# The norm that closes a wide feed-forward block, turned token tile by token tile, and the mixer's first projections taken slice by slice

## What is computed

```python
def _rms(x, g):
    xf = x.astype(jnp.float32)
    y = xf * lax.rsqrt(jnp.mean(xf * xf, axis=-1, keepdims=True) + EPS)
    return y.astype(x.dtype) * g

def _modulate(xn, shift, scale):
    return xn * (1.0 + scale) + shift
...
x = x + 0.5 * ml[:, 2] * _swiglu(_modulate(_rms(x, ffn1_norm[l]), ml[:, 0], ml[:, 1]), ffn1_w_in[l], ffn1_w_out[l])
h = h + 0.5 * mc[2] * _swiglu(_modulate(_rms(h, ffn1_norm[l]), mc[0], mc[1]), ffn1_w_in[l], ffn1_w_out[l])
y_c, y_l = _token_mix(_modulate(_rms(h, mix_norm[l]), mc[3], mc[4]),
                      _modulate(_rms(x, mix_norm[l]), ml[:, 3], ml[:, 4]),
                      mix_w_in[l], mix_b_in[l], ...)
```

## Time and profile before

| | |
|---|---|
| median of three timed runs | 2366.07 us (2363.42 to 2366.50) |
| span of the profiled execution | 2361.7 us |
| TensorE busy | 98% of the span |
| VectorE, ScalarE, GpSimd busy | 67%, 48%, 1% |
| DMA | 403.75 MB, 171 GB/s over the span |

### The profile page before, as it was taken

How to read it: one execution, slowest core, us unless ns; L and a number is a source line. 1 busy time by engine, 2 the same in 40 slices (tenths; PEclk the granted TensorE clock), 3 DMA queues, 4 the chain that set the end, 5 groups by cost and what they waited for, 6 DMA issues and landing times.

```text
span 2361.7 us, 32897 instructions
## 1 busy us (share of the span) xinstructions
PE 2319.4 (98%) x13270; PEld 1954.3 (83%) x13270; DVE 1584.7 (67%) x2393; ACT 1137.5 (48%) x1666; POOL 24.9 (1%) x65
## 2 busy tenths in 40 slices
PE   7999999999999999999999999999999999999998
PEld 4887887888888887888888888888888888888887
DVE  4677434657575777667776678676676676776766
ACT  4222223436434255445545468654464446875444
POOL 0001000010000000000000000000000000000000
PEclk9999999999999999999999999999999999999999
DMA  7468322434522234654555644455555555444553
GB/s 306 179 233 323 139 89 95 150 113 143 195 90 72 73 111 166 241 183 174 194 183 193 236 154 144 157 178 195 183 180 192 196 195 209 149 145 172 188 195 125
DMA packets 59311, 403.75 MB, mean 171 GB/s; under 512 B 8269, under 2 KB 8677, under 8 KB 11672
## 3 DMA queue, kind: packets, MB, share of 16 engines
q1 hardware_dynamic: 52704, 383.80, 45.3%
q10 hardware_dynamic: 4128, 9.95, 1.2%
q0 software_dynamic: 2336, 7.96, 1.1%
HBM read 400.60 MB, written 2.67 MB: 171 GB/s over the span
## 4 chain that ended last, share of the span: by engine, by line
PE 93%; DVE 3%; DMA 2%; ACT 1%; issue 1%; SPq 0%; DVEq 0%; ACTq 0%
PE pair L522 88%; DMA ring<-in_stream 2%; PE pair L904 1%; PE pair L620 1%; PE pair L1050 1%; DVE ring_parts L2346 1%; PE pair L853 0%; ACT xT L1533 0%; PE pair L1319 0%; PE pair L1334 0%; PE pair L892 0%; DVE rows L2463 0%; PE pair L1304 0%; DVE ring_parts L2336 0%; DVE X L2469 0%
## 5 line engine op out<-in xcount | busy, mean ns | idle before, releaser
L522 PE MATMUL pair<-xT_parts,ring_high 128*128 128x512 f32 x2112 | 747.6, 395 | 3.8 <-DVE xT_parts L2251 1.2
L522 PE MATMUL pair<-xT_parts,ring_parts 128*128 128x256 f32 (+2 forms) x2448 | 693.1, 298 | 4.7 <-DVE ring_parts L2346 3.1
L2336 DVE TENSOR_TENSOR ring_parts<-ring,ring_high 128x2048 fp32r<-128x2048 f32 x194 | 444.1, 2292 | 136.4 <-ACT ring_high L1590 136.3
L522 PEld LDWEIGHTS pair<-xT_parts,ring_parts 128*128 128x128 f32 (+1 forms) x2448 | 460.4, 188 | 45.8 <-issue 9.2
L522 PEld LDWEIGHTS pair<-xT_parts,ring_high 128*128 128x128 f32 x2112 | 384.5, 188 | 81.3 <-issue 2.0
L1590 ACT ACTIVATE ring_high<-ring 128x2048 fp32r<-128x2048 f32 x197 | 375.6, 1910 | 67.4 <-DMA ring<-in_stream 67.3
L2346 DVE TENSOR_TENSOR ring_parts<-ring,mix_high 128x1024 fp32r<-128x1024 f32 x144 | 169.2, 1218 | 37.5 <-ACT mix_high L1603 37.5
L1641 ACT ACTIVATE arena<-pair 128x512 f32<-128x512 f32 x110 | 65.6, 596 | 261.9 <-PE pair L522 261.9
L1603 ACT ACTIVATE mix_high<-ring 128x1024 fp32r<-128x1024 f32 x144 | 143.3, 1048 | 93.0 <-DMA ring<-in_stream 89.6
L522 PE MATMUL pair<-ring_parts,xT_parts 128*128 128x512 f32 (+1 forms) x448 | 173.9, 388 | 0.6 <-DVE ring_parts L2346 0.6
L522 PE MATMUL pair<-ring_parts,g_high 128*128 128x512 f32 x440 | 172.2, 391 | 0.2 <-issue 0.2
(11 more groups left out here) (432 smaller groups left out, 3863.6 us busy)
## 6 DMA issues: line engine op xcount, KB each, us to landing
ring<-in_stream SPq DMA_DIRECT2D x338, 1024.0 KB, 4.8
xn<-in_mods SPq DMA_DIRECT2D x14, 1024.0 KB, 4.8
arena<-in_mods SPq DMA_DIRECT2D x14, 1024.0 KB, 4.8
gateB<-gate_rows POOLq DMA_DIRECT2D x4, 512.0 KB, 7.6
xn<-maximum_rows POOLq DMA_DIRECT2D x8, 256.0 KB, 3.6
arena<-in_bT ACTq DMA_DIRECT2D x1, 1536.0 KB, 9.7
bias_scratch<-bias_row POOLq DMA_DIRECT2D x1, 1536.0 KB, 9.1
X<-in_x ACTq DMA_DIRECT2D x1, 1024.0 KB, 11.9
```

The source lines that it names most:

```text
L522: m = pe.matmul(o, l, r, start=start, stop=stop)
L2336: dve.tensor_tensor(out=ring_r[:, slot].rearrange("p a b -> p (a b)"), in0=w, in1=high[:, slot, :], op=ALU.subtract).then_inc(low_ready, 1)
```

## The change

What it does:

- TensorE turns the closing norm by token tile (`norm_wide_by_tile`). Tile 0's slices that land in free banks go first, as soon as tile 0's diagonal is there; those whose bank still held a down product follow with the next tiles. Tile 3 comes last, slice 0 to 7, and its matmuls raise `x_turned`.
- VectorE interleaves reciprocals and diagonals with the last updates: tile 0's behind update (1, 1) (second half row, tile 1), tile 1's behind (1, 2), tile 2's and tile 3's behind (1, 3).
- The high and low part of the mixer's first weight chunk are made before the updates, in the last step of the feed-forward part.
- Part 0 of the first projection group runs slice by slice, all four feature tiles for each slice, and waits for one more slice each time; for slice 0 it waits before each bank until ScalarE has read that bank.

```diff
+            def norm_wide_by_tile():
+
+                first = c.resid - 3
+                for t_, slices in enumerate((((0, 4), (0, 5), (0, 6), (0, 7), (0, 0), (0, 1)),
+                                             ((0, 2),) + tuple((1, k) for k in (4, 5, 6, 7, 0, 1, 2)),
+                                             ((0, 3), (1, 3)) + tuple((2, k) for k in range(KD)),
+                                             tuple((3, k) for k in range(KD)))):
+                    pe.wait_ge(rstd_done, c.rstd + t_ + 1)
+                    pe.wait_ge(resid, first + min(t_ + 1, 3))
+                    for u, k in slices:
+                        m = pe.matmul(bank[k][:, u * P:(u + 1) * P], X[:, u, k * P:(k + 1) * P], diag[:, u, :],
+                                      start=True, stop=True)
+                        if t_ == 3:
+                            m.then_inc(x_turned, 1)
+                        elif owed:
+                            m.then_inc(owed.pop(), 1)
+                c.rstd += 4
+                c.split += KD
...
-                pre_group(range(4), x=both, span=2 * S, turned=c.split, between=gates)
+                pre_group(range(4), x=both, span=2 * S, turned=c.split, between=gates, by_slice=True)
...
-                    if turned is not None:
+                    if turned is not None and (part or not by_slice):
                         pe.wait_ge(x_split, turned - (0 if part else 2 if span == S else CW))
-                    for b, at in fs:
+                    for k in range(CW if by_slice and part == 0 else 0):
+                        pe.wait_ge(x_split, turned - KD + k + 1)
+                        for n, (b, at) in enumerate(fs):
+                            if k == 0:
+                                pe.wait_ge(x_whole, turned - KD + n + 1)
+                            wl, wh = mix_weights(k, slice(at, at + rows), True)
+                            mm(b[0:rows, 0:span], wl, whole[:, k, 0:span], k == 0, False)
+                            mm(b[0:rows, 0:span], wh, rest[:, k, 0:span], False, False)
+                            mm(b[0:rows, 0:span], wh, whole[:, k, 0:span], False, False)
+                    for b, at in fs if part or not by_slice else ():
...
             ffn(4)
-            norm_wide()
+            norm_wide_by_tile()
...
+                        if i == FT // 2 - 1:
+                            mix_split(-1, 0)
...
-                 first_ahead, lambda: mix_split(-1, 0))
+                 first_ahead)
...
+            def diagonals(nt):
 
                 for t_ in rstds(nt):
                     dve.tensor_scalar(diag[:, t_, :], ident[:, :], rstd[:, t_:t_ + 1], None,
                                       ALU.mult).then_inc(rstd_done, 1)
+                    yield t_
...
+                        if i == FT // 2 - 1:
+                            mix_low(-1, 0)
...
+                rooted_tile = diagonals(nt)
                 for n in range(2):
                     for t_ in range(nt):
                         if (n, t_) == (1, 1):
...
                         update(t_, n, down_bank(nt, t_, n), None)
+                        if nt == 4 and n and t_:
+                            next(rooted_tile)
+                if nt == 4:
+                    next(rooted_tile)
...
-            norm(4, lambda: mix_low(-1, 0))
+            norm(4, rooted_before=True)
```

More of the change, by code:

```diff
@@ L1147, in pre_group @@
             def pre_group(features, tokens=(), rows=P, cols=None, width=N, x=None, span=S, turned=None, between=None,
-                          first=None, beside=None):
+                          first=None, beside=None, by_slice=False):
                 whole, rest = x or x_parts
@@ L2233, in rstds @@
                     yield t_
-            def norm(nt, ahead=None):
+            def diagonals(nt):
                 for t_ in rstds(nt):
@@ L2239, in norm @@
                                       ALU.mult).then_inc(rstd_done, 1)
+                    yield t_
+            def norm(nt, ahead=None, rooted_before=False):
+                for t_ in () if rooted_before else diagonals(nt):
+                    pass
                 if ahead:
```

## The result

| | before | after |
|---|---|---|
| median of 21 runs each, in turn on one chip | 2364.47 us | 2367.55 us |
| ratio (95% interval) | | 1.0016 (1.001 to 1.0022) |
| span of the profiled execution, its own time | 2361.7 | 2364.9, 2366.61 |

The change makes the kernel about 3 us slower. The forecast was 1.70 us faster; its range ended at 2367.4, and it gave "same" 0.88. The median lies just outside that range. The ratio's interval lies almost wholly within the 0.2% that the forecast called the limit of measurement, but with 21 runs on each side it excludes 1.

What follows compares the result with a forecast made beforehand. TensorE, 93% of the chain, bounds the kernel; only its 2.73 us idle at this boundary could be won. Projections starting at 416.47 instead of 418.17 save 1.70 us, taking 2366.07 to 2364.4 us; range 2361.2 to 2367.4.

Steps and rivals of the forecast that it cites:

- the gain is carried to the end: Once VectorE waits for TensorE again, by 433.1, all engines keep their distances and the 1.70 us won stays.
- Waiting for each slice costs nothing visible: Part 0 of the projections: slices follow every 1.06 us, TensorE uses 2.75 us for each, so it never waits again.
- The purse and the new order: Between last down products and projections TensorE idles 2.73 us; the new order starts projections at 416.47, not 418.17.
- Slice 0 was the limit: The norm ends at 415.45, but slice 0's low part holds the projections until 416.47.
- Either part alone: Norm by tile without slices one by one starts projections 1.4 us later than before; slice by slice alone wins nothing.
- `gates()` and the backlog: VectorE finishes the gate weights' low part by 425.95; TensorE wants it after part 0, at 427.47: margin 1.5 us.
- Rival 1: Later slices push VectorE's backlog into TensorE and the gain is swallowed: 2366.1 us, chance 0.12.
- Rival 2: Steps between VectorE and ScalarE run 0.3 to 0.5 us longer, so tiles 1 to 3 wait: 2365.4 us, chance 0.10.
- Rival 3: Slice 0 is there when the norm ends, winning the 2.73 us idle: 2363.3 us; chance 0.11 for more than 2.4.
- Rival 4: TensorE's clock falls to its lower level, part 0's 48 matmuls take 11.0 us more: 2375.4 us, chance 0.05.
- the 4.4 us "around" the span: Time outside the profiled span of 2361.7 us, taken as untouched, leading to the median of 2366.07 us.
- later waits for weights that grow by what was won: Sign of a wrong forecast: later in the program, TensorE's waits for weights grow by the 1.70 us gained.

Runs made afterwards that it cites:

- before_8w: Kernel before plus 16 TensorE waits on a value long reached (8 instructions) ahead of the gate products; 2372.11 us, ratio 1.0035 to before.
- after_m8: Changed kernel without 8 needless TensorE waits in the wide part's down steps, same work and order; 2363.42 us, ratio 0.9994 to before.
- before_32w: Kernel before plus 64 TensorE waits on a value long reached (32 instructions) ahead of the gate products; 2366.12 us, ratio 1.0011 to before.
- before_8w_mid: Kernel before plus 16 satisfied TensorE waits (8 instructions) between the two later layers; 2367.03 us, ratio 1.0014 to before.
- before_8w_end: Kernel before plus 16 satisfied TensorE waits (8 instructions) behind the last layer; 2364.82 us, ratio 1.0005 to before.
- tile3_early: Changed kernel with 16 fewer instructions and the norm's last pieces reordered so slice 0 is whole earlier; 2360.65 us, ratio 0.9991 to before.
- tile_only: Changed kernel with part 0 of the projections again after all four slices, and 8 needless waits fewer; 2367.51 us, run once.
- after_again: Changed kernel once more, nothing edited; 2369.90 us, ratio 1.0027 to before.
- before_8w_again: Repeat of the kernel before plus 16 satisfied TensorE waits (8 instructions) at 427 us; 2371.55 us, ratio 1.0026 to before.
- before_m8: Kernel before without 8 needless TensorE waits in the wide block's down steps; 2362.83 us, ratio 1.0000 to before.

## Why the prediction was wrong

The direction was wrong, and the step that failed is one sentence: "From there on all engines wait on each other with the same distances, and the gain is carried to the end, 1900 us further." Measured, the 1.9 us won at the boundary were outweighed by 3.07 us of later landings and 2.3 of lowered clock in the profile. The sentence on the waits, "Waiting for each slice costs nothing visible", was right only at the place itself.

- *The distances between engines* stayed the same next to the boundary (-2.03 at 419, -2.02 at 917). What did not stay is the distance between TensorE's demand for its own program and SyncE's weight transfers. The 8 more instructions, all waits, brought the packets of the program up to 1.6 us nearer to the issues of the transfers on which TensorE waits. One of the sixteen marks that end a transfer then comes 1.4 us behind the others (5.77 against 4.38), and the landing is some 1.2 later. Shown: the same effect with 8 waits that do nothing (before_8w), its end at once when 8 are taken out (after_m8), when 32 carry the packets past (before_32w), and its change with the place within one kernel (before_8w_mid, before_8w_end).
- *The purse and the new order*: idle 2.73; forecast 1.70 won, measured 1.9 (2.03 in starts, 0.15 of it an earlier arrival). Diagonals, squares and roots came within 0.2 of their times relative to the stretch. Slice 0 was the limit, by an idle time of 0.74 where 1.02 was worked out (416.47 - 415.45). Most of that difference is bookkeeping: the row of 7.30 holds the pipeline's depth, and from start to start the 64 pieces take 7.06 (tile3_early), not 7.19, which by the same count makes the wait 0.98. Against the stretch ScalarE's first modulated piece came 0.15 sooner than worked out.
- *Either part alone*: forecast -1.4 and 0, measured -1.3 and 0.
- *`gates()` and the backlog*: forecast at 427.47 with a margin of 1.5; measured at 427.15, no wait, the low part started at 424.42.
- *Rival 1*, the swallowed gain, had VectorE's backlog as its mechanism; that did not occur. *Rival 2*, diagonals late: did not occur. *Rival 3*, the whole purse: not in after, but in tile3_early. *Rival 4*: in the profile of after the clock stayed at 1.00 through part 0, 48 matmuls from 416.14 to 427.15, 0.229 each, and cycling through four banks did not slow it, so the rule of the Trainium skill that was weighed there ("TensorE: Matmul & The Clock Gate", "A second HAM failure mode: psum-queue depth-cycling") does not show here. The argument against this rival was weaker than it looked, though: the profile of before had 1.00 behind its idle time of 1.91 at 410.31, but in seven of the nine profiles with that norm (all but before and before_8w) the clock falls to its lower level at 411 to 412, which costs 1.0 to 1.6. In none of the eight with the new norm and slices one by one does it fall there; in six of them it falls at 917 to 922, which costs 0.7 to 1.0 (in three of the nine with the old norm, at 923 or 924). In tile_only, with 3.93 idle ahead of part 0, it falls at 420. One profile of before didn't show this.
- *The span against the time*: the 4.4 us "around" the span were misread. Runs with both numbers show 1.7 between them (2366.61 and 2364.9), so the profile of before belongs to an execution of 2363.4, quicker than the median of the three timed runs by 2.7 and than that of the 21 by 1.1. That left the forecast difference untouched, but it understated how much of a profile is the execution's own luck.
- The forecast did name, under what would show it wrong, "later waits for weights that grow by what was won". They grew by more than was won, and not from the earlier arrival: after_m8 arrives as early and has none.

What stays open: lowered clock. In 16 of the 18 profiles it falls in one to six short stretches behind 400 us, at places that differ between executions of one kernel (it starts at 411 to 420, 917 to 924, 1333 to 1369 or 1957 to 1998), and one costs up to 3.2 us. The runs of before in the last two groups with a mean clock of 0.999 take 2360.7 to 2361.8, those with 0.993 or 0.994 take 2365.0 to 2366.5. The mean clock of the runs of before and after_again is nearly the same (0.9959 and 0.9956), so this makes the scatter and not the sign. Four late transfers give 5.0 us directly and about 7 in the mean. That they draw more lowered clock behind them would fill the gap; it is argued from before_8w_again's profile, not shown. The mean clock doesn't tell it: at 0.993 or 0.994 four executions with 8 waits took 2372.2 to 2374.2, some 7 to 8 us more than before at the same clock. The +2.8 of before_32w, without a late transfer, is open in the same way. Nor did I derive why a packet so far ahead of the landing, at 0.9 us, is late while one at 0.4 mostly is not.

## What to carry to other kernels

Count the instructions that a change adds to the busiest engine, waits too: its program comes over the same DMA engines as the weights, and where a transfer is on the chain, a packet of 16 KB beside it was a cost of 1.2 us here, some 900 us and more behind the edit. Before judging an edit of one or two us, run it beside a version with the same number of instructions, by taking out needless waits or adding empty ones; a sign that turns with that says nothing about the edit. Needless waits are not worth taking out for their own sake: before_m8 gained nothing by it.

## What the runs showed of the hardware

- TensorE's program arrives in 105 packets of 16 KB, 257 instructions each, of about 0.96 us, each at a place in the instruction stream that shifts with the number of instructions ahead. One that starts 0.9 to 4.0 us behind the issue of a 1 MB transfer delays its landing from 4.7 to 5.0 to some 5.9 to 6.4 us; in after 15 of the 16 marks that end the transfer are on time, and the last is 1.4 us behind them.
- 8 instructions of satisfied waits beside TensorE's 26,948: +7.6 and +7.2 us of 2363 at one place (427 us), with no delay at the place itself; +0.9 (interval includes 0) at the end, +3.3 between; 32 instructions at the first place: +2.8 (before_32w).
- 64 matmuls of 128x128 over 8 banks, in an order given by when their inputs come, followed each other every 0.110 us (7.06 from the first start to the next matmul's in tile3_early); in bank order in before it was 0.112 (58 in 6.52).
